# One-hots in two instructions, eight places for the rows of the second matrix, and own places for its activations and products

## What is computed

```python
def chunk_fn(hc):                                   # 128 positions
    q = (hc @ wq).reshape(t, 8, 2, 128)
    s = einsum("thpk,pnk->thpn", q, sk)
    s1, i1 = top_k(s[:, :, 0], 16); s2, i2 = top_k(s[:, :, 1], 16)
    cand = (s1[..., :, None] + s2[..., None, :]).reshape(t, 8, 256)
    best, j = top_k(cand, 16)
    e = take(i1, j // 16) * 128 + take(i2, j % 16)
    gate = softmax(best)
    act = gelu(einsum("thkd,td->thk", u_tab[e], hc))
    return einsum("thk,thkd->td", gate * act, v_tab[e])
...
x = x + g1 * mixer(modulate(rms_norm(x)))
x = x + g2 * peer(modulate(rms_norm(x)))
```

## Time and profile before

| | us |
|---|---|
| median of 3 runs (3136.67 to 3146.48) | 3139.86 |
| the profiled execution, time | 3141.54 |
| its span | 3139.8 |
| PE busy | 2904.3 (93%) |
| DVE busy | 2430.9 (77%) |
| POOL busy | 1424.9 (45%) |
| ACT busy | 1207.3 (38%) |
| `oh_c` L995, 96 times, mean 2033 ns | 195.2 |
| `oh_i` L996, 96 times, mean 702 ns | 67.4 |
| `oh_j` L999, 288 times, mean 735 ns | 196.9 |
| a gate store, 4096 KB, from issue to landing | 16.1 |

### The profile page before, as it was taken

How to read it: one execution, slowest core, us unless ns; L and a number is a source line. 1 busy time by engine, 2 the same in 40 slices (tenths; PEclk the granted TensorE clock), 3 DMA queues, 4 the chain that set the end, 5 groups by cost and what they waited for, 6 DMA issues and landing times.

```text
span 3139.8 us, 50852 instructions
## 1 busy us (share of the span) xinstructions
PE 2904.3 (93%) x15754; PEld 2554.2 (81%) x15754; DVE 2430.9 (77%) x4532; ACT 1207.3 (38%) x1590; POOL 1424.9 (45%) x878
## 2 busy tenths in 40 slices
PE   5888999999998899999899899999999989999997
PEld 3657999989888788888777689989888878888885
DVE  7965679999995688888765307799999937888887
ACT  2333333345553333333333324333555523333332
POOL 2623367776667122222324244777766651222221
PEclk8999999999999999999999899999999989999998
DMA  6336567779898899999935124777788898999996
GB/s 240 134 128 221 199 206 240 242 263 349 308 350 321 301 353 350 355 356 352 351 122 174 66 100 138 229 251 239 277 328 328 310 348 308 352 353 351 357 347 232
DMA packets 352434, 849.74 MB, mean 271 GB/s; under 512 B 30048, under 2 KB 194016, under 8 KB 350176
## 3 DMA queue, kind: packets, MB, share of 16 engines
q1 hardware_dynamic: 239888, 479.53, 44.5%
q0 software_dynamic: 73728, 268.47, 23.6%
q10 hardware_dynamic: 38736, 100.84, 8.1%
HBM read 741.76 MB, written 106.95 MB: 270 GB/s over the span
## 4 chain that ended last, share of the span: by engine, by line
PE 54%; DVE 21%; issue 11%; POOL 7%; DMA 4%; ACT 1%; SPq 0%; POOLq 0%; DVEq 0%; ACTq 0%
PE bank L1418 11%; PE bank L1419 11%; PE bank L1420 11%; POOL w_lo L407 6%; DVE oh_c L995 5%; DVE oh_j L999 5%; PE bank L1360 4%; PE bank L1362 4%; PE bank L1361 4%; DVE rows L1160 2%; PE bank L1260 2%; PE bank L1262 2%; PE bank L1261 2%; DVE oh_i L996 2%; DMA x<-u_rows,u_idx 1%
## 5 line engine op out<-in xcount | busy, mean ns | idle before, releaser
L407 POOL TENSOR_TENSOR w_lo<-w_raw,w_hi 128x1024 fp32r<-128x1024 f32 x338 | 838.6, 2481 | 694.1 <-ACT w_hi L517 692.2
L517 ACT ACTIVATE w_hi<-w_raw 128x1024 fp32r<-128x1024 f32 x594 | 629.1, 1059 | 1346.3 <-PE bank L1420 668.6
L1360 PE MATMUL bank<-h_hi,w_hi 128*128 128x384 f32 x2048 | 702.7, 343 | 42.5 <-POOL w_lo L407 29.8
L1362 PE MATMUL bank<-h_lo,w_hi 128*128 128x384 f32 x2048 | 688.9, 336 | 0.0
L1361 PE MATMUL bank<-h_hi,w_lo 128*128 128x384 f32 x2048 | 688.3, 336 | 0.0
L461 POOL DMA_INDIRECT shared<-stream,v_idx x256 | 246.8, 964 | 830.9 <-DVE rows L1069 746.6
L1418 PE MATMUL bank<-w_hi,h_hi 128*128 128x512 f32 x1536 | 600.7, 391 | 16.6 <-ACT h_hi L642 14.3
L1419 PE MATMUL bank<-w_hi,h_lo 128*128 128x512 f32 x1536 | 600.0, 391 | 0.0
L1420 PE MATMUL bank<-w_lo,h_hi 128*128 128x512 f32 x1536 | 599.8, 390 | 0.0
L1039 DVE TENSOR_TENSOR w_lo<-w_raw,w_hi 128x1024 fp32r<-128x1024 f32 x256 | 313.7, 1226 | 199.9 <-ACT w_hi L517 199.0
L1360 PEld LDWEIGHTS bank<-h_hi,w_hi 128*128 128x128 f32 x2048 | 387.1, 189 | 58.9 <-issue 55.9
(11 more groups left out here) (193 smaller groups left out, 3584.6 us busy)
## 6 DMA issues: line engine op xcount, KB each, us to landing
w_raw<-stream SPq DMA_DIRECT2D x600, 512.0 KB
act_dram<-act_words ACTq DMA_DIRECT2D x256, 192.0 KB
gate_dram<-shared ACTq DMA_DIRECT2D x12, 4096.0 KB, 16.1
act_words<-act_dram SPq DMA_DIRECT2D x256, 192.0 KB
shared<-gate_dram SPq DMA_DIRECT2D x128, 384.0 KB
oh_j<-mod_rows SPq DMA_DIRECT2D x60, 512.0 KB, 4.7
oh_i<-mod_rows SPq DMA_DIRECT2D x20, 512.0 KB, 5.4
shared<-mod_rows SPq DMA_DIRECT2D x16, 512.0 KB, 14.0
```

The source lines that it names most:

```text
L407: nc.gpsimd.tensor_tensor(lo_of(grp, s), w_raw[:, s, :], hi_of(grp, s).bitcast(F32), ALU.subtract).then_inc(S["lo_ready"], 1)
L517: nc.scalar.activation(hi_of(grp, s), w_raw[:, s, :], ACT.Copy).then_inc(S["hi_ready"], 1)
L1360: MM(o, hi, h_hi[:, k, P:T], start=(k == 0), stop=False)
L1362: ins = MM(o, hi, h_lo[:, k, P:T], start=False, stop=(k == KC - 1))
```

## The change

- The one-hots take two instructions: one compare writes `oh_c` and the `oh_i` of this group (`oh_ic`, three places, taken with a step), one multiply writes all three `oh_j`. Keys and gate parts are laid out by group for it. The multiply waits for the compare directly.
- The first set of early dots is gone: 18 early dots for 36. `dots_to(g)` is 18 + 2g for 36 + g + (g + 1) // 2. In a group the dots stand ahead of the one-hots. POOL's row fetches of the retrieval are one a tile in tiles 3 to 8 of a block.
- The reloaded activations have own places (`act_v`), and the first four loads wait for the first store of their place, not for the last. The products of the second matrix go to columns 0 to 127 of `h_hi` and `h_lo` (`product`), which expert tiles don't read.
- ACT applies Gelu to the dots, and makes the first product, inside its step of the last expert tile, so it waits there for all dots. DVE makes the first two gated products ahead of the first `w_low`, and the weights before `w_low` of tile 1.
- Rows of the second table have eight places. `axpy` n stands behind tile n, from tile 0.

```diff
@@ -80,16 +80,16 @@
 SLOTS = HEADS * TOPK
 GROUPS = DT // GROUP
 U_RING = 6
-V_RING = 4
+V_RING = 8
 EARLY_SET = U_RING
-EARLY = 2 * DB * EARLY_SET
+EARLY = DB * EARLY_SET
 def dots_to(g):
-    return EARLY + g + (g + 1) // 2
+    return EARLY + 2 * g
...
@@ -235,10 +235,11 @@
         scores = part(8192, TB, 2 * HEADS, NK)
         gate_st = part(0, 2, NK, HALF)
         g_ring = part(0, RING // 2, DT // HALF, 2 * HALF)
-        prod = part(2048, 2, DT)
+        prod = part(1536, 2, DT)
+        act_v = part(2304, RING, DT)
         mod_b_ring = [oh_words[:, i * D:(i + 1) * D] for i in range(3)]
-        mod_b_ring.append(oh_i[:].rearrange("p a b c d -> p (a b c d)").bitcast(F32))
-        v_row_ring = part(8192, V_RING, D)
+        mod_b_ring.append(oh_i.rearrange("p a b c d -> p (a b c d)").bitcast(F32))
+        v_row_ring = part(4096, V_RING, D)
         v_out = part(12288, TB, D)
         def u_row(n):
...
@@ -273,6 +274,10 @@
         def glu_in(c, which):
             return (z, z_more)[c // 2][:, 2 * (c % 2) + which, :]
+        def product(h, s):
+            return h[:, DB * (s % 2):DB * (s % 2) + DB, 0:P]
         def out_bank(m, n):
             return 2 * ((m + 1) % DB) + n
...
@@ -370,7 +375,7 @@
                     sp.wait_ge(g_st[r], 16 * ((l + 1) * DB + 1))
                 for s in range(RING):
-                    sp.wait_ge(act_st[s], 16 * (l + 1) * EXPERT_TILES // RING)
+                    sp.wait_ge(act_st[s], 16 * (l * EXPERT_TILES // RING + 1))
                     load_products(0, s)
                     if s < 2:
                         load(first, s + 2)
...
@@ -381,6 +386,8 @@
                         sp.wait_ge(S["p_ready"], i * RING + (l * EXPERT_TILES + s - RING + 1))
                         load_products(i, s)
+                for s in range(RING):
+                    sp.wait_ge(act_st[s], 16 * (l + 1) * EXPERT_TILES // RING)
                 with sp.Fori(1, EXPERT_TILES // RING) as i:
                     expert_loads(i)
                 sp.wait_ge(S["dot"], (l + 1) * SLOTS)
...
@@ -479,8 +486,7 @@
                     b, r = g // TILES_PER_BLOCK, g % TILES_PER_BLOCK
                     group = g - TB * TILES_PER_BLOCK - RING
                     if b < TB:
-                        end = 2 * (b - 1) * EARLY_SET + min(max(r - 1, 0), EARLY_SET) + (
-                            EARLY_SET if r == TILES_PER_BLOCK - 1 else max(r - 10, 0))
+                        end = (b - 1) * EARLY_SET + min(max(r - 2, 0), EARLY_SET)
                     elif group < GROUPS:
                         end = min(dots_to(max(group - 1, 0)) + U_RING, n + 2)
                     else:
...
@@ -654,9 +661,9 @@
                         prod_hi(i, s + 1)
                         make_hi(i + v_first, s + 2)
-                next_tiles(0)
-                act.wait_ge(S["dot"], (l + 1) * SLOTS)
-                nc.scalar.activation(dots[:], dots[:], ACT.Gelu).then_inc(S["dot_act"], 1)
+                for s in range(RING):
+                    prod_hi(0, s + 1, s == 0)
+                    make_hi(v_first, s + 2)
                 with act.Fori(1, last) as i:
                     next_tiles(i)
                 for s in range(RING):
...
@@ -846,16 +853,13 @@
                 LINKS = 20
-                def early_dots(b, half):
-                    if isinstance(b, int):
-                        return
+                def early_dots(b):
                     for r in range(EARLY_SET):
-                        had = l * len(range(r, SLOTS, U_RING)) - 2 + half + 1
-                        dve.wait_ge(u_ld[r], b * 32 + 16 * had)
+                        had = l * len(range(r, SLOTS, U_RING))
+                        dve.wait_ge(u_ld[r], b * 16 + 16 * had)
                         V.scalar_tensor_tensor(out=u_row(r), in0=u_row(r), scalar=1.0, in1=rows[:], op0=ALU.mult,
-                                               op1=ALU.mult, accum_out=dots[:, bass.ds(b * 2 * EARLY_SET
-                                                                                       + (half - 2) * EARLY_SET + r, 1)]
+                                               op1=ALU.mult, accum_out=dots[:, bass.ds(b * EARLY_SET + r - EARLY_SET, 1)]
                                                ).then_inc(S["dot"], 1)
                 def retrieve(b, plus, fetched):
...
@@ -958,10 +961,11 @@
                     dve.wait_ge(S["tr_mm"], b + l * DB)
                     at = (b - 1) * P
-                    V.tensor_copy(i_t[:, bass.ds(at, P)], ps[4][:, 0:P])
-                    V.tensor_copy(j_t[:, bass.ds(at, P)], ps[4][:, P:2 * P])
+                    for w in range(2):
+                        V.tensor_copy(keys_t[:, bass.ds((b - 1) * (P // GROUP), P // GROUP), w, :],
+                                      ps[4][:, w * P:(w + 1) * P].rearrange("p (g t) -> p g t", t=GROUP))
                     chained(V.tensor_copy(gate_t[:, bass.ds(at, P)], ps[4][:, 2 * P:3 * P]))
-                    early_dots(b, 1)
+                    early_dots(b)
                 retrieve(0, 0, True)
                 dve.wait_ge(S["ht_ready"], l + 1)
...
@@ -974,30 +978,32 @@
                 chain[0] = base + DB * LINKS
                 for part_no in range(3):
-                    link(V.tensor_copy(gate_p[:, part_no, :], gate_t[:]))
+                    left = gate_t[:].rearrange("p (g t) -> p g t", t=GROUP)
+                    link(V.tensor_copy(gate_p[:, :, part_no, :], left))
                     if part_no < 2:
-                        link(V.tensor_tensor(gate_t[:], gate_t[:], gate_p[:, part_no, :], ALU.subtract))
+                        link(V.tensor_tensor(left, left, gate_p[:, :, part_no, :], ALU.subtract))
                 groups = l * GROUPS
                 def of_group(t, g):
-                    return t[:, g * GROUP:(g + 1) * GROUP].rearrange("p (a b) -> p a b", b=2).unsqueeze(2
-                                                                     ).to_broadcast([P, PAIR, NK, 2])
+                    n = t.shape[2]
+                    return t[:, g, :, :].rearrange("p n (a b) -> p (n a) b", b=2).unsqueeze(2
+                                                                   ).to_broadcast([P, n * PAIR, NK, 2])
                 def one_hots(g):
                     s = g % 2
-                    keys = iota_2[:].unsqueeze(1).to_broadcast([P, PAIR, NK, 2])
+                    keys = iota_2[:].unsqueeze(1).to_broadcast([P, 2 * PAIR, NK, 2])
                     if groups + g >= 2:
                         dve.wait_ge(S["g_mm"], 2 * (groups + g) - 2)
                     if groups + g:
                         dve.wait_ge(S["oh_ready"], groups + g)
-                    V.tensor_tensor(oh_c[:], keys, of_group(j_t, g), ALU.is_equal).then_inc(S["oh_cmp"], 1)
-                    V.tensor_tensor(oh_i[:, s, :, :, :], keys, of_group(i_t, g), ALU.is_equal)
+                    V.tensor_tensor(oh_ic[:, s:3:2 - s, :, :, :], keys, of_group(keys_t, g), ALU.is_equal
+                                    ).then_inc(S["oh_cmp"], 1)
                     dve.wait_ge(S["oh_cmp"], groups + g + 1)
-                    for w in range(3):
-                        ins = V.tensor_tensor(oh_j[:, s, w, :, :, :], oh_c[:], of_group(gate_p[:, w, :], g), ALU.mult)
-                    ins.then_inc(S["oh_ready"], 1)
+                    V.tensor_tensor(oh_j[:, s, :, :, :, :], oh_c.unsqueeze(1).to_broadcast([P, 3, PAIR, NK, 2]),
+                                    of_group(gate_p, g), ALU.mult).then_inc(S["oh_ready"], 1)
                 def dot(n):
                     r = n % U_RING
...
@@ -1006,9 +1012,9 @@
                                            op1=ALU.mult, accum_out=dots[:, n:n + 1]).then_inc(S["dot"], 1)
                 for g in range(GROUPS):
-                    one_hots(g)
                     for n in range(dots_to(g), dots_to(g + 1)):
                         dot(n)
+                    one_hots(g)
                 for n in range(dots_to(GROUPS), SLOTS):
                     dot(n)
...
@@ -1040,14 +1046,17 @@
                                     ).then_inc(S["lo_ready"], 1)
+                gated(0, 0, True)
+                gated(0, 1, True)
                 dve.wait_ge(S["lo_ready"], first)
                 w_low(0, 0)
-                gated(0, 0, True)
-                w_low(0, 1)
-                gated(0, 1, True)
                 prod_lo(0, 0)
                 gated(0, 2)
+                dve.wait_ge(S["dot_act"], l + 1)
+                V.tensor_tensor(dots[:], dots[:], gate_0[:], ALU.mult).then_inc(S["weight"], 1)
+                w_low(0, 1)
                 prod_lo(0, 1)
+                dve.wait_ge(S["weight"], l + 1)
                 last = EXPERT_TILES // RING - 1
                 def two_ahead(i, s, tiles=RING):
...
@@ -1058,35 +1067,32 @@
                     if s + 3 < tiles:
                         gated(i, s + 3)
-                def axpy(i, s, begin=False):
-                    dve.wait_ge(v_ld[s], i * 16 + l * 16 * SLOTS // V_RING)
```

(60 more changed lines are left out.)

12 lines of the change are left out of this document (5 added, 7 removed).

## The result

The changed kernel takes 3217.21 us (median of 3 runs, 3215.34 to 3218.68), against 3139.86: a ratio of 1.0242, 95% interval 1.0215 to 1.027, so it is slower by 77 us. The forecast of 3186 us had the sign and the place, and was 31 us too low; the time lies inside the range of 3092 to 3230.

A forecast was written before the change was run, and what follows sets the result against it. No engine is full over the span, PE nearest; in the groups DVE partly waits for POOL. Terms -3 + 90 - 3 - 17 - 7 - 14 = +46 on 3141.5 gave 3187.5, so forecast 3186 us, range 3092 to 3230.

The forecast's parts named there:

- Rival (1): Group stage: rows keep up beside a store, latency under 8 us; the +90 is gone, 3096 us; chance 0.20.
- Rival (2): One-hots on DVE: wider patterns lose the double pace, 5120 elements take 5.3 us, kernel 3300 us; chance 0.05.
- The price of a store: Group stage: late rows beside gate stores cost 9 us a store, five stores a layer, +90; ends 5 and 11.
- my 2 us for the clock: Group stage: 2 us added to each store's cost because PE restarts at a low clock after a gap.
- three groups at PE's pace: Group stage: after each store's stall the next three groups run at PE's pace, -1.5 us a store.
- The one-hots: Group stage: two instructions save 9 us, fourteen groups falling into the late mode cost 6; sum -3.
- Retrieval: Retrieval blocks: six dots and their waits removed, fewer PE stalls; -8.4 us a layer, -17 together, ends -6 and -28.
- The second matrix: Tail of the groups and second matrix, both layers: -24 us predicted.
- The end: End of the second matrix: the last four weighted rows no longer come behind the last tile; -9.8 and -4.3, -14 us.
- The head: Start of the second matrix: earlier loads and products shorten PE's wait; 7.7 us lost a layer, sum -7, ends -14, +6.
- the contention term: Start of the second matrix: four more row fetches, 2 MB or 6 us of DMA at 354 GB/s, charged as 3.5.
- The rule that takes turns: Group stage: DMA engines alternate between queues, so rows arrive a few us late at most, +90 near nothing; judged contradicted.

The follow-up runs named there:

- the split: The changed kernel with each 4 MB gate store issued as four stores of 1 MB, one every second group: 3103.99 us, ratio 0.987.
- 1/8 store: The changed kernel storing only one eighth of the gates at each store and reading that part back for all: 3095.74 us, ratio 0.9843.
- the one that took 3071.8: The changed kernel with the row dots' old schedule (36 early, 1.5 a group, behind the one-hots) and gate stores in four parts: 3071.8 us, ratio 0.9768.
- old dots: The changed kernel with the row dots' old schedule (36 early, 1.5 a group, behind the one-hots), stores whole: 3109.71 us, ratio 0.9916.

## Why the prediction was right, and where it was short

**The place and the mechanism held.** Five stores a layer with a stall, rows 17 us behind a fetch next to a store (16.91 and 17.83; 17.3 predicted), DVE waits of 8.0 to 8.8 at nine of ten (7 to 10), PE stalls of the same size, groups otherwise 6.1 to 6.2 apart, one-hots 2.88 behind `w_lo` (711.79 to 714.67; 2.8 to 2.9). Rival (1) needed a latency under 8 us beside a store; the split and the cut stores show its world, 3104 and 3096, where it put 3096. Rival (2) is out: 1.22 and 1.76 us for 2048 and 3072 elements without a wait are 2.98, where it had 5.3.

**The price of a store was the term that was mis-sized.** With the 1/8 store as the base, a store costs (345.1 + 344.8 - 290.6 - 290.7) / 10 = 10.9 us, not 9: +109 for +90, at the upper end given (11). The intervals from the first store on are 15.15, 7.63, 5.62, 5.62 and 7.66, against 6.18 each with the 1/8 store: 10.8 more. The first is the stall (+9.0), the second the low clock behind it (+1.5; from 738 to 748 the granted clock is 0.87), and with my 2 us for the clock these two are about what I had worked out. I had credited 1.5 for three groups at PE's pace; two of them come, -1.1. The fifth interval is the one I did not have (+1.5): a second row is late, 36 us after the store was issued. Seven of the ten stores have such a second wait, of 3.4 to 4.2 us (timeline of the changed kernel):

```profile
745.17 3.53 POOL L414 TENSOR_TENSOR w_lo<-w_raw,w_hi 128x1024 fp32r<-128x1024 f32 x1 [10.15 <-ACT w_hi L523]
...
748.84 1.82 POOL L458 DMA_INDIRECT u_more<-u_rows,u_idx  x1
...
755.85 1.22 DVE L1011 SCALAR_TENSOR_TENSOR u_more<-u_more,rows 128x1024 f32<-128x1024 f32 x1 [4.22 <-DMA u_more<-u_rows,u_idx]
```

This row was no slower than others: 7.01 from fetch to use, 6.45 for a row. It was fetched late. Its place in the ring was free at 737.13, but POOL's program has the fetch behind the low part of the next tile, and that tile came late because PE had stood. So the stall comes back once through POOL. Over the window that answers to the earlier trace rows the granted clock is 0.94 where it was 1.00.

```profile
800.00:900.00 100.00, 84.66 (x687) 81.00 (x686) 84.90 (x84) 49.27 (x57) 74.13 (x41) 0.94 0.79 282
```

**The one-hots**: -3 predicted, +1.8 here (290.65 a layer with the 1/8 store, against 289.75 before). Alone they gave 5.2 us of the span. Two dots a group use up what they save.

**Retrieval**: -17 predicted, -19.9. Blocks 2 and 3 of layer 0 last 68.5 and 68.6 (69 to 70), block 1 gained nothing (-1), and 1.6 were lost ahead of the first group.

**The second matrix**: -24 with the tail predicted, -13.5. The end did what was said (gaps of 12.12 and 6.63 in the earlier trace rows became 2.17 and none). The head did not:

```profile
1083.60 0.56 DVE L1031 TENSOR_TENSOR shared<-shared 128x384 f32<-128x384 f32 x1 [9.64 <-DMA shared<-gate_dram]
...
1086.11 0.77 PE L1424 MATMUL bank<-w_hi,h_hi 128*128 128x512 f32 x1 [6.03 <-DVE h_lo L1039]
...
2668.41 0.77 PE L1424 MATMUL bank<-w_hi,h_hi 128*128 128x512 f32 x1 [7.83 <-DVE h_lo L1039]
```

A first gap of 2.50 stands in each layer, as worked out, and then these, 6.03 and 7.83, where I had charged 3.5 for the loads behind the rows. The gaps of the earlier trace rows, 9.57 and 4.68, have become 8.5 and 10.3: the loads start earlier, but into a queue that eight row fetches fill. The step that failed is the contention term, sized by bandwidth (2 MB at 354 GB/s) and then halved. The load of 384 KB issued at 1068.31 landed 15.2 us later, behind six of the eight rows (the other two landed at 1084.49 and 1086.67). It is cut into 768 packets of 512 bytes, and those of the rows are 4 KB; that it waits for the rows' larger packets in turn fits, and is not tested.

**The rule that takes turns.** The Trainium skill (DMA: Bandwidth & Descriptors, section Queues, rings and completion order) has each DMA engine alternate between queues. I took the 17.3 us as evidence against it, and that was the wrong reading. The trace agrees that turns are taken: beside the first store 128 packets of the store, 136 of gathered rows and 137 of loads start in the same 12.7 us. What I had left out is that a turn of the store was 32 KB and 1.23 us long, and a turn of the row 4 KB and 0.16. The forecast did not hang on this, since it took the latency itself from the earlier trace rows.

## What to carry to other kernels

Before a consumer is moved closer to its fetch, compare the slack that the ring leaves (here 8 to 9 us) with the latency measured beside the largest transfer (16.9), not with the mean latency; if it is shorter, cut that transfer up before anything else, and look at the size of its packets. Put what the bottleneck engine needs ahead of what can be late in each queue. And a saving on an engine at 100% busy is worth reading twice: part of that share may be waiting for another engine, as the compare here for POOL's `w_lo`.

## What the runs showed of the hardware

- A gathered row (512 KB in packets of 4 KB) took 9.6 to 10.4 us from fetch to use beside a store of 1 MB in packets of 8 KB, and 16.9 to 18.6 beside nine of ten stores of 4 MB in packets of 32 KB, at the same total of bytes. Beside the first such store, packets of the three queues started about one for one. Behind the groups, where POOL has several rows in flight, rows took 9.6 to 18.1 with the parts too.
- A bf16 compare of 128 x 2048 takes 1.22 us by itself and 2.1 to 3.5 behind a POOL `TENSOR_TENSOR` of 2.4, ending 1.1 behind it each time (changed kernel and the one that took 3071.8). One program (old dots) held 5.62 us a group through one layer and 6.2 from the twelfth interval on in the other; DVE busy shares of 99.4% stand at 5.62 and at 6.0 us a group.
- A POOL row fetch takes 0.95 us by itself, mostly 1.47 to 1.83 beside the long one-hot instructions (some 2.3), and 1.23 beside the short ones in the earlier trace rows.
